# Down projection's last two output blocks in two passes over token halves, with the norm and the index projection by halves

## Chip, core and metric

The kernel runs on one core of one Trainium2 chip. The metric is the device time of one launch in microseconds, the median of several runs. Lower is better.

## What is computed

Two layers of a decoder trunk over 512 tokens of width 1024. Cut to what matters here:

```
for i in range(2):
    h = x @ w_in                      # index, query, key/value, conv and gate projections
    ... three mixers, gates, output projection ...
    x = layer_norm(ALPHA * x + merged @ w_out, ln1_g, ln1_b)
    f_gate, f_up = split(x @ w_ffn_in)            # 1024 -> 2 x 2816
    ffn = (silu(f_gate) * f_up) @ w_ffn_out       # 2816 -> 1024, "down"
    ple = sigmoid(x @ w_ple_gate) * (p_i @ w_ple_proj)
    x = layer_norm(ALPHA * x + ffn + ple, ln2_g, ln2_b)   # "norm 2"
```

All is float32. The norm is over the 1024 channels of a token, so a token's result needs all eight output blocks of the down projection, but no other token.

## The kernel before

**Layout.** The residual `u` and its split copies `xh`, `xl` are held channels on partitions: eight blocks (`DK` = 8) of 128 channels x 512 tokens. Each float32 product is made of three matmuls in the round float format: high x high, high x low, low x high (`three`, L775 to L777; for projections that put tokens on partitions L826 to L828). So every weight is needed as a high and a low part, and every activation too.

**Weight feed.** All weights come as a list of tiles of 128 x 1024 (512 KB), `TILES` = 152 a layer, in the order in which TensorE uses them. SP loads tile t into `wraw[t % 2]` (L411) once POOL is through with tile t-2 (`lo_ready`). ACT rounds it to `wh[t % 4]` (`high`, L489) once TensorE has used tile t-4 (`tile_used`) and the load has landed. POOL makes `wl[t % 4]` = raw - high (`low`, L443), and TensorE waits for that (`arrived`). Each engine runs its list in order. ACT's list has the roundings between its other work: at step k of a stage it rounds the tile three ahead (`LEAD`).

**Down projection.** The 22 input blocks (`FK`) of `hh`, `hl` times the weights of output block j; j runs from 0 to 7. Each j has three tiles (8, 8 and 6 blocks of 128 x 128, the third filled up with zeros), 24 tiles in all. Output block j goes to PSUM bank 2 + j % 2, all 512 tokens at once, and DVE adds it to `u` (`arrive`, L1319).

**Norm 2.** After j = 3 a shift is taken from the first blocks (`shift`, bank 0) and subtracted. DVE keeps a running sum over blocks (L1355), ACT squares each block (`squares`, L578), DVE adds the squares (`add_square`, L1325; both inputs in SBUF). After block 7, TensorE forms per token mean and mean square (`by_token`, L981), spreads the mean to all partitions (L991), DVE and ACT make 1/deviation (`deviation`), DVE puts it on a diagonal (L1379), TensorE spreads it (L995). Then DVE goes through the blocks: scale (L1391, the factor in PSUM), centre (L1367, the mean in PSUM) and, after ACT has made `xh` (`norm_high`, L590), the low part `xl` (L1397, all inputs in SBUF). In the last layer ACT writes the result to `u` (L767) and SP stores each block as it comes.

ACT's squares of blocks 0 to 3 stand in its list at tile step 12 of the down projection; the fourth of them waits for an add of DVE that comes after the sum of block 4.

**Index projection.** The first four tiles of a layer: 2 channel blocks a tile, 452 columns, for all four blocks of 128 tokens, 96 matmuls. TensorE waits for `xl` block by block (`x_ready`).

## Time and profile before

| | us |
|---|---|
| median of 3 runs | 1916.29 (1915.11 to 1917.13) |
| the profiled execution, its own time | 1914.98 |
| its span in the profile | 1913.2 |
| TensorE busy | 1861.6 (97%) |
| VectorE (DVE) busy | 1008.0 |
| ScalarE (ACT) busy | 732.6 |
| GpSimd (POOL) busy | 748.3 |

The profile is of one execution. Times are from the span's start. The median is that of unprofiled runs. A matmul's duration overlaps the next one's, so its pace is read from starts. The granted clock of TensorE is 0.992 of full speed on average. Of DMA, 163.6 MB are weight tiles.

### The profile page before, as it was taken

What the parts mean: (1) busy time and instruction counts of PE and PEld (TensorE: products, weight loads), DVE (VectorE), ACT (ScalarE), POOL (GpSimd) and SP (SyncE); (2) the same over time, 40 slices, a digit from 0 to 9 for tenths busy, and PEclk for the clock granted to TensorE, in tenths of its full rate; (3) what the DMA queues carried; (4) which work ended last, traced back from release to release, by engine and by line L of the source; (5) the groups of instructions that cost most, each with busy time, mean ns of one, the idle gap of its engine ahead of it and who ended that gap; (6) DMA issues with size and microseconds to landing.
All of it is one profiled execution on the core that took longest, in us unless ns stands there. A gap on an engine that the chain in (4) does not pass through costs nothing.

```text
span 1913.2 us, 25744 instructions
## 1 busy us (share of the span) xinstructions
PE 1861.6 (97%) x9076; PEld 1542.2 (81%) x9076; DVE 1008.0 (53%) x1875; ACT 732.6 (38%) x1253; POOL 748.3 (39%) x318
## 2 busy tenths in 40 slices
PE   8999999999999999999999999999999999999996
PEld 8888788878778888887798887888777788888875
DVE  5388777848974121112253987777589731111023
ACT  4544455543242222222344445455433332222222
POOL 4443212234445444443533532222344544444432
PEclk9999999999999999999999999999999999999998
DMA  5322111122233332332332321111132333323322
GB/s 179 100 91 87 45 56 56 56 67 88 89 99 99 99 99 91 97 108 72 121 97 88 100 78 45 56 54 58 56 99 89 110 99 98 97 90 99 103 88 74
DMA packets 47032, 166.07 MB, mean 87 GB/s; under 512 B 5472, under 2 KB 5728, under 8 KB 46944
## 3 DMA queue, kind: packets, MB, share of 16 engines
q1 hardware_dynamic: 46080, 163.60, 27.4%
q10 hardware_dynamic: 864, 1.28, 0.2%
q8 instruction: 58, 0.95, 0.2%
q14 instruction: 30, 0.25, 0.0%
HBM read 162.76 MB, written 2.10 MB: 86 GB/s over the span
## 4 chain that ended last, share of the span: by engine, by line
issue 67%; POOL 28%; PE 2%; POOLq 1%; DVE 1%; DMA 0%; ACT 0%; SPq 0%; DVEq 0%; ACTq 0%
POOL sb_wl L443 28%; PE banks L777 1%; PE banks L775 1%; PE banks L776 1%; POOLq L442 0%; POOLq L452 0%; DMA sb_wraw<-in_weights 0%; DVE sb_u L1391 0%; DMA sb_u<-in_x 0%; DVE sb_u L1367 0%; PE banks L995 0%; PE banks L981 0%; POOL sb_wl L447 0%; ACT sb_u L767 0%; ACT sb_wh L489 0%
## 5 line engine op out<-in xcount | busy, mean ns | idle before, releaser
L443 POOL TENSOR_TENSOR sb_wl<-sb_wraw,sb_wh 128x1024 fp32r<-128x1024 f32 x303 | 745.0, 2462 | 1125.3 <-ACT sb_wh L489 1125.1
L775 PE MATMUL banks<-sb_xh,sb_wh 128*128 128x512 f32 x1344 | 548.0, 408 | 2.8 <-POOL sb_wl L443 1.8
L777 PE MATMUL banks<-sb_xh,sb_wl 128*128 128x512 f32 x1344 | 524.9, 391 | 0.0
L776 PE MATMUL banks<-sb_xl,sb_wh 128*128 128x512 f32 x1344 | 524.4, 390 | 0.0
L489 ACT ACTIVATE sb_wh<-sb_wraw 128x1024 fp32r<-128x1024 f32 x303 | 318.9, 1055 | 263.8 <-PE banks L777 146.9
L777 PEld LDWEIGHTS banks<-sb_xh,sb_wl 128*128 128x128 f32 x1344 | 252.2, 188 | 53.9
L775 PEld LDWEIGHTS banks<-sb_xh,sb_wh 128*128 128x128 f32 x1344 | 253.0, 188 | 51.9 <-issue 5.1
L776 PEld LDWEIGHTS banks<-sb_xl,sb_wh 128*128 128x128 f32 x1344 | 253.5, 189 | 40.0
L1249 DVE SCALAR_TENSOR_TENSOR banks<-sb_hconv,sb_par,banks 128x512 f32<-128x512 f32 x232 | 173.9, 750 | 0.8
L775 PE MATMUL banks<-sb_hh,sb_wh 128*128 128x512 f32 x352 | 138.6, 394 | 2.1 <-POOL sb_wl L443 2.1
L777 PE MATMUL banks<-sb_hh,sb_wl 128*128 128x512 f32 x352 | 138.4, 393 | 0.0
L776 PE MATMUL banks<-sb_hl,sb_wh 128*128 128x512 f32 x352 | 137.3, 390 | 0.0
L1319 DVE TENSOR_TENSOR sb_u<-sb_u,banks 128x512 f32<-128x512 f32 x32 | 21.9, 686 | 201.5 <-PE banks L777 201.3
L1596 DVE TENSOR_TENSOR sb_th<-sb_th,banks 128x512 f32<-128x512 f32 x44 | 30.3, 688 | 175.8 <-PE banks L777 175.8
L1593 DVE SCALAR_TENSOR_TENSOR sb_th<-sb_th,banks 128x512 f32<-128x512 f32 x44 | 30.3, 688 | 158.2 <-ACT sb_th L493 158.2
L534 ACT ACTIVATE sb_ptbuf<-banks 128x128 f32<-128x128 f32 (+3 forms) x128 | 55.9, 437 | 135.7 <-PE banks L882 135.5
L749 ACT ACTIVATE sb_hh<-sb_th 128x512 f32 x44 | 27.8, 632 | 204.1 <-DVE sb_th L1596 204.1
L493 ACT ACTIVATE sb_th<-banks 128x512 f32<-128x512 f32 x60 | 35.9, 598 | 176.0 <-PE banks L777 175.9
L826 PE MATMUL banks<-sb_wh,sb_xh 128*128 128x452 f32 (+3 forms) x256 | 90.3, 353 | 6.2 <-DVE sb_xl L1397 3.5
L827 PE MATMUL banks<-sb_wl,sb_xh 128*128 128x452 f32 (+3 forms) x256 | 90.1, 352 | 0.0
L828 PE MATMUL banks<-sb_wh,sb_xl 128*128 128x452 f32 (+3 forms) x256 | 89.8, 351 | 0.0
L775 PEld LDWEIGHTS banks<-sb_hh,sb_wh 128*128 128x128 f32 x352 | 66.1, 188 | 17.2 <-issue 3.4
(273 smaller groups left out, 2876.9 us busy)
## 6 DMA issues: line engine op xcount, KB each, us to landing
sb_wraw<-in_weights SPq DMA_DIRECT2D x304, 512.0 KB, 3.5
sb_u<-in_x SPq DMA_DIRECT2D x8, 256.0 KB, 6.2
out<-sb_u SPq DMA_DIRECT2D x8, 256.0 KB, 2.0
sb_praw<-in_ple ACTq DMA_DIRECT2D x2, 512.0 KB, 3.9
sb_par<-in_params ACTq DMA_DIRECT2D x2, 98.5 KB, 1.9
sb_rope_tmp<-in_freq ACTq DMA_DIRECT2D x1, 24.0 KB, 4.2
sb_small<-in_pos ACTq DMA_DIRECT2D x1, 2.0 KB, 3.9
```

The source lines that it names most:

```text
L443: nc.gpsimd.tensor_tensor(wl[:, t % WS, :], wraw[:, t % 2, :], wh[:, t % WS, :].bitcast(F32), ALU.subtract).then_inc(lo_ready, 1)
L489: nc.scalar.activation(wh[:, t % WS, :], wraw[:, t % 2, :], ACT.Copy).then_inc(hi_ready, 1)
L493: nc.scalar.activation(dst, psum[:, bank, :], ACT.Tanh, scale=0.5, bias=bias).then_inc(done, 1)
L534: nc.scalar.activation(ptbuf[:, n % 2, 0:w], psum[:, bank, 0:w], ACT.Copy).then_inc(turn_out, 1)
L775: nc.tensor.matmul(out, wh_, xh_, start=start, stop=False)
L776: nc.tensor.matmul(out, wh_, xl_, start=False, stop=False)
L777: return nc.tensor.matmul(out, wl_, xh_, start=False, stop=stop)
L826: nc.tensor.matmul(o, th_, h[:, kk], start=(k == 0), stop=False)
L827: nc.tensor.matmul(o, th_, lw[:, kk], start=False, stop=False)
L828: last = nc.tensor.matmul(o, tl_, h[:, kk], start=False, stop=(k == nk * tiles - 1))
L1249: steps.done(v.scalar_tensor_tensor(acc, h, w, acc, ALU.mult, ALU.add))
L1593: steps.done(v.scalar_tensor_tensor(tc, tc, 1.0, psum[:, 4 + 2 * c, :], ALU.add, ALU.mult))
```

## The change

In each layer the down projection does output blocks 0 to 5 as before (`WHOLE` = 6). Blocks 6 and 7 are done twice over, first for tokens 0 to 255 (22 input blocks for j = 6, 22 for j = 7, 256 columns a matmul), then for tokens 256 to 511. Their weights are in the list twice. Tiles are filled without gaps over the whole list: 220 blocks, 28 tiles, the last with 4 blocks. `TILES` becomes 156.

The second pass uses other banks (4, 5). The norm of half 0 is placed beside it: TensorE has `half_sums` after matmul block 185 and `half_spread` after block 197 of the second pass (blocks 176 to 219). ACT does the half squares at tile steps 20, 22 and 27 of its list, the root at step 23, and the high parts of half 0 two at a time at steps 24 to 27, each behind that step's rounding. DVE goes through half 0 and does the addition of block 6, half 1, in between (`OTHER_AT`). Half 1 follows.

In the second layer the index projection runs by halves, all four tiles for half 0, with the sums and the spread of half 1 after its first and second tile, and then all four tiles, which stay in SBUF, for half 1. The output is stored in 16 pieces.

```diff
+HALVES = 2
+HALF = S // HALVES
+WHOLE = DK - 2
+DOWN = [(j, k, None) for j in range(WHOLE) for k in range(FK)]
+DOWN += [(j, k, half) for half in range(HALVES) for j in range(WHOLE, DK) for k in range(FK)]
+DOWN_TILES = -(-len(DOWN) // DK)
+DOWN_AT = {(j, half): n for n, (j, k, half) in enumerate(DOWN) if k == FK - 1}
+SQUARES_AT = {11: (0, 1, 2, 3), 14: (4,), 17: (5,)}
+HALF_SQUARES_AT = {20: ((6, 0),), 22: ((7, 0),), 27: ((6, 1),)}
+SUMS_AT, SPREAD_AT = DOWN_AT[(DK - 1, 0)] + 10, DOWN_AT[(DK - 1, 0)] + 22
+OTHER_AT = 5
+TILES = T_FO + DOWN_TILES
...
+            for half in range(HALVES):
+                for j in range(DK):
+                    sp.wait_ge(z_full, DK * half + j + 1)
+                    sp.dma_start(out[:, j, columns_of(half)], u[:, j, columns_of(half)]).then_inc(out_stored, 16)
...
-                for k in range(PARTS * DK):
+                for k in range(DOWN_TILES):
                     if T_FO + k + LEAD < TILES or layer < L - 1:
                         high(T_FO + k + LEAD, first)
...
+                    for jj in SQUARES_AT.get(k, ()):
+                        squares(layer, 1, jj)
+                    for j, half in HALF_SQUARES_AT.get(k, ()):
+                        squares_of_half(layer, j, half)
+                    if k == DOWN_TILES - 5:
+                        deviation(layer, 1, 0)
+                    if k >= DOWN_TILES - 4:
+                        for j in range(2 * (k - DOWN_TILES + 4), 2 * (k - DOWN_TILES + 4) + 2):
+                            norm_high(layer, 1, j, 0)
+                squares_of_half(layer, DK - 1, 1)
+                deviation(layer, 1, 1)
                 if layer < L - 1:
                     high(LEAD, first + TILES)
...
+                for j in range(DK):
+                    norm_high(layer, 1, j, 1)
...
+            def index_by_halves(layer, first):
+
+                name, ncol, nk, tiles = TOKEN_GROUPS[0]
+                for half in range(HALVES):
+                    for t in range(tiles):
+                        if half == 0:
+                            arrived(t, first)
...
+                        for kk in range(nk):
+                            k = nk * t + kk
+                            pe.wait_ge(x_ready, split_at(layer - 1, 1, half) + (DK + k + 1))
+                            for b in range(2 * half, 2 * half + 2):
...
+                        if half == 1:
+                            last.then_inc(tile_used, 1)
+                        elif t == 0:
+                            half_sums(layer - 1, 1)
+                        elif t == 1:
+                            half_spread(layer - 1, 1)
...
+            def half_sums(layer, half):
+
+                at, c, blocks = stat(layer, 1, half), columns_of(half), range(2 * half, 2 * half + 2)
+                by_mean, by_square = [psum[:, 2 + 2 * half + i, 0:2] for i in range(2)]
+                pe.wait_ge(sum_ready, at + 1)
+                by_token(by_mean, sums[1][:, 0], blocks).then_inc(mean_ready, 1)
+                pe.wait_ge(sq_half_summed, layer * 2 * HALVES + (2 * half + 2))
+                by_token(by_square, sums[1][:, 1], blocks).then_inc(sq_ready, 1)
+                nc.tensor.matmul(psum[:, STAT[1], c], ones_d[:], sums[1][:, 0, c], start=True,
+                                 stop=True).then_inc(mean_spread, 1)
...
+                for n, (j, k, half) in enumerate(DOWN):
+                    t, c = T_FO + n // DK, slice(n % DK * P, n % DK * P + P)
+                    if n % DK == 0:
+                        arrived(t, first)
...
+                    if half is None:
+                        bank, src_h, src_l = psum[:, 2 + j % 2, :], hh[:, k], hl[:, k]
+                    else:
+                        bank = psum[:, 2 + 2 * half + j % 2, 0:HALF]
+                        src_h, src_l = hh[:, k, columns_of(half)], hl[:, k, columns_of(half)]
+                    last = three(bank, wh[:, t % WS, c], wl[:, t % WS, c], src_h, src_l, k == 0, k == FK - 1)
...
+                    if n == SUMS_AT:
+                        half_sums(layer, 0)
+                    if n == SPREAD_AT:
+                        half_spread(layer, 0)
...
+                    for j in range(DK + 1):
+                        if j < DK:
...
+                            v.scalar_tensor_tensor(u[:, j, c], u[:, j, c], column("l2g", j), scale, ALU.mult,
+                                                   ALU.mult).then_inc(z_ready, 1)
+                            if j + EARLY < DK:
+                                center(j + EARLY)
+                        if j >= 1 and layer < L - 1:
+                            dve.wait_ge(x_high, z0 + (DK + j))
+                            v.scalar_tensor_tensor(xl[:, j - 1, c], u[:, j - 1, c], column("l2b", j - 1),
+                                                   xh[:, j - 1, c].bitcast(F32), ALU.add, ALU.subtract).then_inc(x_ready, 1)
+                        if j == OTHER_AT:
+                            steps.wait()
+                            other()
...
+                add_square(WHOLE - 1)
+                for j in range(WHOLE, DK):
+                    arrive(j, 0)
+                for j in range(WHOLE, DK):
+                    add_square_of(j, 0)
+                chain(0, lambda: arrive(WHOLE, 1))
+                arrive(DK - 1, 1)
+                for j in range(WHOLE, DK):
+                    add_square_of(j, 1)
+                chain(1, lambda: None)
```

## Rows read from the trace of the kernel before

**Rows 1.** The page: busy time of each engine, and POOL's step of the feed.
```profile
PE 1861.6 (97%) x9076; PEld 1542.2 (81%) x9076; DVE 1008.0 (53%) x1875; ACT 732.6 (38%) x1253; POOL 748.3 (39%) x318
...
L443 POOL TENSOR_TENSOR sb_wl<-sb_wraw,sb_wh 128x1024 fp32r<-128x1024 f32 x303 | 745.0, 2462 | 1125.3 <-ACT sb_wh L489 1125.1
```
**Rows 2.** Timeline of TensorE, end of the first layer (start, duration, what, idle before).
```profile
946.22 0.40 PE L777 MATMUL banks<-sb_hh,sb_wl 128*128 128x512 f32 x1
...
950.30 2.05 PE L991 MATMUL banks<-sb_sums,sb_ones_d 128*128 128x512 f32 x2
...
957.63 0.72 PE L826 MATMUL banks<-sb_wh,sb_xh 128*128 128x452 f32 x1 [3.53 <-DVE sb_xl L1397]
...
963.05 0.43 PE L828 MATMUL banks<-sb_wh,sb_xl 128*128 128x452 f32 x1
...
979.69 0.36 PE L828 MATMUL banks<-sb_wh,sb_xl 128*128 128x452 f32 x1
```
**Rows 3.** Timeline of TensorE and DVE, end of the second layer.
```profile
1893.38 0.40 PE L777 MATMUL banks<-sb_hh,sb_wl 128*128 128x512 f32 x1
...
1895.28 1.95 PE L981 MATMUL banks<-sb_ones_d,sb_sums 128*128 128x1 f32 x16 [1.51 <-DVE sb_sums L1355]
...
1897.09 1.11 PE L991 MATMUL banks<-sb_sums,sb_ones_d 128*128 128x512 f32 x2
...
1898.82 2.07 PE L995 MATMUL banks<-sb_sums,sb_ones 128*128 128x512 f32 x2 [0.63 <-DVE sb_sums L1379]
1901.01 0.75 DVE L1391 SCALAR_TENSOR_TENSOR sb_u<-sb_u,sb_par,banks 128x512 f32<-128x512 f32 x1 [1.05 <-PE banks L995]
...
1908.56 1.40 DVE L1391 SCALAR_TENSOR_TENSOR sb_u<-sb_u,sb_par,banks 128x512 f32<-128x512 f32 x2
```
**Rows 4.** Timeline of TensorE, after the tile waits and in a 256-column projection.
```profile
906.53 0.47 PE L775 MATMUL banks<-sb_hh,sb_wh 128*128 128x512 f32 x1 [1.04 <-POOL sb_wl L443]
...
998.00 0.28 PE L826 MATMUL banks<-sb_wh,sb_xh 128*128 128x256 f32 x1
...
1009.51 0.40 PE L826 MATMUL banks<-sb_wh,sb_xh 128*128 128x512 f32 x1
```
**Rows 5.** Timeline of POOL from 900 to 970.
```profile
911.30 2.41 POOL L443 TENSOR_TENSOR sb_wl<-sb_wraw,sb_wh 128x1024 fp32r<-128x1024 f32 x1 [2.55 <-ACT sb_wh L489]
915.14 2.41 POOL L443 TENSOR_TENSOR sb_wl<-sb_wraw,sb_wh 128x1024 fp32r<-128x1024 f32 x1 [1.43 <-ACT sb_wh L489]
...
933.28 2.67 POOL L443 TENSOR_TENSOR sb_wl<-sb_wraw,sb_wh 128x1024 fp32r<-128x1024 f32 x1 [1.07 <-ACT sb_wh L489]
...
968.93 4.88 POOL L443 TENSOR_TENSOR sb_wl<-sb_wraw,sb_wh 128x1024 fp32r<-128x1024 f32 x2 [14.51 <-ACT sb_wh L489]
```
**Rows 6.** Timeline of ACT where it stands before the fourth square.
```profile
902.34 0.63 ACT L578 ACTIVATE sb_sq<-sb_u 128x512 f32<-128x512 f32 x1 [14.46 <-DVE sb_sums L1325]
902.88 1.99 ACT L489 ACTIVATE sb_wh<-sb_wraw 128x1024 fp32r<-128x1024 f32 x2
```
**Rows 7.** Timeline of DVE beside POOL, in norm 2 and norm 1.
```profile
932.99 3.50 DVE L1325 TENSOR_TENSOR sb_sums<-sb_sums,sb_sq 128x512 f32<-128x512 f32 x2
...
533.54 2.40 POOL L443 TENSOR_TENSOR sb_wl<-sb_wraw,sb_wh 128x1024 fp32r<-128x1024 f32 x1 [4.47 <-ACT sb_wh L489]
...
534.47 2.02 DVE L1397 SCALAR_TENSOR_TENSOR sb_xl<-sb_u,sb_par,sb_xh 128x512 fp32r<-128x512 f32 x1
```
**Rows 8.** Stretches of TensorE (busy of PE, PEld, DVE, ACT, POOL, granted clock, DMA).
```profile
958.00:962.00 4.00, 4.00 (x12) 3.51 (x12) 4.00 (x8) 1.45 (x2) 0.00 (x0) 0.50 0.00 0
```
**Rows 9.** Groups of DVE by shape (busy, mean ns, idle before).
```profile
L1325 DVE TENSOR_TENSOR sb_sums<-sb_sums,sb_sq 128x512 f32<-128x512 f32 x28 | 29.5, 1053 | 2.1 <-DVE sb_sums L1325 0.5 <-ACT sb_sq L578 0.2
...
L1319 DVE TENSOR_TENSOR sb_u<-sb_u,banks 128x512 f32<-128x512 f32 x32 | 21.9, 686 | 201.5 <-PE banks L777 201.3
...
L1461 DVE SCALAR_TENSOR_TENSOR sb_scores<-sb_relu,sb_small,sb_scores 128x512 f32<-128x512 f32 x6 | 4.5, 752 | 0.6
...
L1461 DVE SCALAR_TENSOR_TENSOR sb_scores<-sb_relu,sb_small,sb_scores 128x256 f32<-128x256 f32 x6 | 2.9, 485 | 0.6
```

More of the change, by code:

```diff
@@ L959, in attention, with by_token @@
                         turn_blocks("out", n, "", [ystage[:, n % 2, b, :] for b in range(NT)], P)
-            def down(t, part, first, bank, start, stop):
-                arrived(t, first)
-                blocks = min(DK, FK - part * DK)
-                for b in range(blocks):
-                    k, c = part * DK + b, slice(b * P, b * P + P)
-                    last = three(psum[:, bank, :], wh[:, t % WS, c], wl[:, t % WS, c], hh[:, k], hl[:, k],
-                                 start and b == 0, stop and b == blocks - 1)
-                last.then_inc(tile_used, 1)
+            def by_token(bank, block, blocks):
+                for i, b in enumerate(blocks):
+                    last = nc.tensor.matmul(bank[:, i:i + 1], block[:, b * P:b * P + P], ones_d[:, 0:1], start=True,
+                                            stop=True)
+                return last
@@ L1023, in _ @@
                         scratch(n, layer)
+                    elif layer > 0 and n < TOKEN_GROUPS[0][3]:
+                        if n == 0:
+                            index_by_halves(layer, first)
                     elif n in tile_group:
@@ L1115, in _ @@
                         project(T_FI + 2 * c + 1, first + i * 4, xh, xl, DK, [5 + 2 * c])
-                for j in range(DK):
-                    pe.wait_ge(u_ready, layer * 16 + (DK + j + 1))
-                    for part in range(PARTS):
-                        pe.wait_ge(h_done, layer * (DK + FK) + (DK + min(DK * (part + 1), FK) + 2))
-                        down(T_FO + PARTS * j + part, part, first, 2 + j % 2, part == 0, part == PARTS - 1)
-                    if j == 3:
-                        shift(layer, 1)
-                norm(layer, 1)
+                down(layer, first)
+                if layer == L - 1:
+                    half_sums(layer, 1)
+                    half_spread(layer, 1)
         @block.vector
@@ L1351, in norm @@
                     steps.wait()
-                for j in range(4, DK):
+                for j in range(4, (DK, WHOLE)[n]):
                     arrive(j)
@@ L1650, in weight_tiles @@
         tiles += [fi[j:j + 1], fi[FK + j:FK + j + 1]]
-    down = w_ffn_out.reshape(FK, P, DK, P).transpose(2, 1, 0, 3)
-    for j in range(DK):
-        for part in range(PARTS):
-            blocks = down[j, :, part * DK:part * DK + DK]
-            tiles.append(padded(blocks.reshape(1, P, -1)))
+    down = w_ffn_out.reshape(FK, P, DK, P).transpose(2, 0, 1, 3)
+    blocks = [down[j, k] for j, k, _ in DOWN]
+    blocks += [np.zeros_like(blocks[0])] * (DK * DOWN_TILES - len(blocks))
+    tiles.append(np.stack(blocks).reshape(DOWN_TILES, DK, P, P).transpose(0, 2, 1, 3).reshape(DOWN_TILES, P, DK * P))
     return np.concatenate(tiles, axis=0)
```

195 lines of the change are left out of this document (132 added, 63 removed).

## Prediction

> **What bounds the kernel now.** I read first the page's busy times [rows 1]. TensorE is busy 97% of 1913.2 us; no other engine is above 53% (the weight loads lie beside the matmuls). So the time is TensorE's stream of matmuls plus its gaps, and the change can win only gaps. POOL's group waits 1125 us, nearly all on ACT's rounding of a weight tile: it is idle, but it is one link of a chain (load, ACT, POOL), and a chain can be slow although none of its links is busy.
>
> Then the timeline of TensorE at the end of the first layer [rows 2]. The last down matmul starts at 946.22 and ends at 946.62; the index projection starts at 957.63, 3.53 of the 11.0 us between being plain idle there, the rest statistics that wait on one another; it ends at 979.9 (the last starts at 979.69 and the next would follow 0.2 later). Its first 14 steps, to 963.05, are 0.387 us each, the 81 from there to 979.69 are 0.205: the granted clock is 0.50 there, 1.2 of 2.4 GHz [rows 8], and costs 14 x 0.182 = 2.6 us. At the end of the second layer the down projection ends at 1893.78 and the span at 1913.2, so 19.4 us of tail [rows 3]. These two stretches are all that the change can shorten.
>
> **Pace of a half matmul.** Durations overlap, so I take starts. A 512-column matmul comes every 0.229 us (173 steps from 906.53 to 946.22, 0.2283 without the first, which is slower) [rows 2, 4]. A 256-column one comes every 0.1199 us (96 steps from 998.00 to 1009.51, in the projection of the key/value rank) [rows 4]. Two halves cost 0.2398 against 0.2283: 0.0115 x 132 (2 blocks x 22 x 3) = +1.5 us a layer. The Trainium skill (TensorE: Matmul & The Clock Gate, Back-to-back issue gap) gives N/2.4 + 2.5 ns, by which the two would cost 2.5 ns more than the whole, +0.3 us a layer; the rows are of this kernel and decide.
>
> **Pace of the weight feed.** This is where the change meets something that it does not name. A tile goes: load, ACT rounds it, POOL subtracts, and only then may the next load into the same of two buffers be issued. When it is starved the feed shows its own pace [rows 5]: seven POOL steps start between 911.30 and 933.28 (three are shown), 22.0 us for six tiles, 3.66 us a tile, 7.33 us for a round of one buffer. POOL is 2.41 of a round, ACT 1.1 (its two at 902.88 take 1.99 [rows 6]); 3.8 pass from POOL's end to the next rounding in that buffer. A tile of 8 whole blocks lasts 8 x 3 x 0.2283 = 5.48 us, and that pace is covered. A tile of half blocks lasts 8 x 3 x 0.12 = 2.88 us: it is not. The change has 11 such tiles in a row, and 28 tiles instead of 24 (4 more loads, 4 more ACT and POOL steps a layer).
>
> Does it enter with tiles in hand? No. Before, ACT stands 14.5 us in front of the fourth square (it waits for an add that comes after block 4), cannot round, and TensorE then waits 1.04 us for a tile [rows 4, 6]. The change keeps this order: the four squares sit behind tile step 11 instead of 12, block 4 ends at matmul block 111 instead of 109. So TensorE again finds an empty hand, two blocks later: at R = 906.53 + 1.37 = 907.9 (the second layer has the same order, and I take the same for it). I count from R.
>
> **Down stage, step by step from R.** Tiles ready (end of POOL's step, every 7.3 us a buffer): 17 at 7.2, 19 at 14.5, 21 at 21.8, 23 at 29.1, 25 at 36.4, 27 at 43.7; even ones 2.4 us behind (16, 18, ... at 2.3, 9.6, 16.9, 24.2, 31.5, 38.8). TensorE: tile 15 to 5.5; tile 16 (4 whole, 4 half blocks) to 9.7; 17 to 20 to 21.2; waits 0.6 for tile 21 and ends the first pass at 24.7; tile 22 to 27.6; waits 1.5 for tile 23; two blocks of it and the column sums bring it to 30.4. There half_sums waits for the squares. The square of block 7 stands on ACT behind the rounding of tile 25 (step 22), whose load could be issued only when POOL was through with tile 23, at 29.1; it rounds at 32.8 to 33.8, squares to 34.2 (a 512-wide square is 0.63 [rows 6]; I shorten it by what DVE gains, below). Then DVE's add.
>
> That add has both inputs in SBUF, and POOL is just then at tile 25. Rows: two such adds from 932.99 took 3.50 us, while POOL ran 933.28 to 935.95, and one is 0.69 alone; a low-part step took 2.02 beside POOL's at 533.54 (0.74 alone) [rows 5, 7]. They end 0.54 after POOL does. Over the whole kernel the add with two SBUF inputs (L1325) takes 1.053 on average, the one with an input in PSUM (L1319) 0.686, which is never held [rows 9]. The Trainium skill (SBUF — State Buffer, "two separate sides") says the same: a DVE op with two SBUF inputs and a GpSimd op lock each other out for the whole instruction. It speaks against this change, which moves a norm from a stretch where POOL is idle (14.5 us before 968.93 [rows 5]) under a stretch where it works two thirds of the time.
>
> So the add ends at 36.7 and TensorE has stood 6.5 us. Before, the clock had fallen 3.7 us after the last dense matmul in one layer and by 5.1 us in the other (pairs at 950.30 and 1898.82 take 2.05, one at 1897.09 takes 1.11), and it came back after 5.4 us of slow work (957.63 to 963.05) [rows 2, 3]. I take the same here: 2.7 us. Statistics in the stream: by token 16 matmuls took 1.95 us at full clock, so 8 take 1.0; each spread pair took 1.1 at 512 columns, so two half ones 1.0 [rows 3]: 2.0 us.
>
> Down stage then ends at 53.4. Whole: 1.5 + 2.0 + feed waits 2.1 + wait for squares 6.5 + clock 2.7 = +14.8 us against R's old end (946.62 - 907.9 = 38.7). Both layers alike.
>
> **First layer, to the end of the index.** Scale of half 0 lands at 45.5. DVE's loop per block (scale 0.40, centre 0.33, low part 0.40, each 0.27 under the 512 one: 752 against 485 ns [rows 9]) would need 9 us alone. But ACT does blocks 2 and 3 only after the rounding of tile 28, 4 and 5 after tile 29, 6 and 7 after tile 30; these take the feed's pace, and each low part has two SBUF inputs. POOL is at tile 28 until 50.7: low part 2 ends at 51.1; at tile 29 from 51.4 to 53.8: low part 3 ends at 54.2, so scale 5 comes at 54.6 and ACT's block 5 at 55.1, and only then the rounding of tile 30 (to 56.1); POOL is at it until 58.6: low part 5 at 59.0, scale 7 at 59.4, low part 7 at 60.4. DVE then adds block 7 of half 1 and its sum: 61.2. TensorE is through with the first index tile at 55.8: it waits 5.4 us, and the clock falls again (2.7). Then statistics 2.0, 0.5 us of waits, the other 84 index matmuls. Down's end to index's end: 96 x 0.205 = 19.7, + 2.0 + 5.4 + 2.7 = 29.8, against 33.3 before (979.9 - 946.6): -3.5. The second half's low parts (from 70.5, one per 1.13 us) are ahead of TensorE, which takes one per 1.23 us. The rounding behind them (tile 4, at 76.7 to 80.2 with POOL) is just in time for 83.2. Net +14.8 - 3.5 = **+11.3 us**.
>
> **Second layer, tail.** No more loads after tile 27, so POOL is quiet. From down's end to the first scale step: 7.2 before (1893.78 to 1901.01); arrival, sum and diagonal lose 0.27 each, by-token and spread matmuls half their 1.95 and 2.07, part of which DVE's steps hid: 5.0. Then eight scale-centre steps of 1.26 (six from 1901.01 to 1908.56), 9.0 with the last two; 0.53 less each: 5.2. ACT's last step and the store, 3.2 to 1913.2, become 2.9; that SP now issues 16 stores, not 8, I cost at nothing, 0 to +0.5. 13.1 against 19.4 [rows 3]: -6.3. Net +14.8 - 6.3 = **+8.5 us**.
>
> **Sum.** +19.8. The profiled execution was 1914.98 us with a span of 1913.2, 1.3 under the median 1916.29. The sum is made on its span and added to the median: 1936.
>
> **Costed at nothing.** h_done and bank waits of the new loop (other banks, tiles 6 to 20 blocks old); norm 1 (same steps); ACT's copies of the index projection, which come up to 2 us later against their matmuls since a rounding stands before them: covered by the next projections, which TensorE has in hand; without that cover +2. If DVE's steps hold POOL's in turn (its mean is 2.462 over all, 2.41 alone [rows 1, 5]), 0.3 a tile over 11 tiles is +3.
>
> **Rivals.**
> (a) The overlap works as written: the feed keeps up and DVE is not held. Then down ends at 38.7 + 1.5 + 2.0 = 42.2 less rounding, index at 63.6 against 72.0 (-8.4), the tail gives -6.3 + 3.5 = -2.8: -11 us, 1905. It decides if a tile can be fed in under about 3 us; against it speaks every starved step in the rows (3.66), for it only that the first pass might find more tiles in hand than I count. 10%.
> (b) The feed is the bound, but the squares come before the clock falls or the holds on DVE are short: no clock term (-8), shorter waits (-5): +5 to +12, 1921 to 1928. For it: two fifths of the DVE steps will fall into POOL's pauses (3.66 less 2.41), and the clock fell after 3.7 us in one layer and 5.1 in the other, so it has no fixed moment. 23%.
> (c) It evens out: gains of the tails (3.5 + 6.3) equal a down stage that is only 5 us longer, within 4 us: 7%.
> (d) Worse: loads land later, as one did (3.84 us between POOL's steps at 911.30 and 915.14, where the other buffer should have followed by 2.4), the round is 7.7, copies of the index delay the rotation: +24 to +32. 12%.
> (e) Forecast: +12 to +24. 48%.
>
> **How the numbers follow.** Left out of 1918 to 1944 are (a), half of (c) and some of (d), 0.18 in all. The likeliest case's own range is 1928 to 1940. A measurement of this kernel can tell about 0.2% (4 us) from no change. Faster by more: (a), 0.10. Within: (c) and the edge of (b), 0.08. Slower: 0.82.
>
> **What would show it.** Right: TensorE idle 0.5 to 1.5 us before tiles 21 and 23 on POOL's step; 5 to 7 us before the by-token matmuls of the squares, released by DVE; slow matmuls after it; POOL's steps every 3.7 us through both passes; half-width adds and low parts of over 1 us; idle of 3 to 6 us after the first index tile; the tail from the last down matmul 13 us. Wrong: POOL's steps at 3 us, no idle in the second pass, or a down stage under 45 us from R.

## The result

| | median | runs | range |
|---|---|---|---|
| before | 1916.71 us | 4 | 1915.11 to 1921.74 |
| changed | 1936.97 us | 4 | 1934.83 to 1940.31 |

The ratio is 1.0109, 95% interval [1.0095, 1.0123]: 20.3 us slower by the medians. The profiled execution of the changed kernel is the 1940.31 one, with a span of 1938.5 us; the other three have spans of 1936.0, 1934.3 and 1933.0.

From its page: the busy times and the group of POOL's step, to be read beside [rows 1].

```profile
PE 1869.7 (96%) x9348; PEld 1563.3 (81%) x9348; DVE 1034.7 (53%) x1937; ACT 747.6 (39%) x1285; POOL 766.7 (40%) x326
...
L467 POOL TENSOR_TENSOR sb_wl<-sb_wraw,sb_wh 128x1024 fp32r<-128x1024 f32 x311 | 763.3, 2458 | 1146.2 <-ACT sb_wh L513 1146.0
```

TensorE has 272 instructions more, and 8 us more of busy time; the rest of the 25.3 us that this execution is longer is idle. Where it lies, the timeline of TensorE shows (start, duration, instruction, idle before it and its releaser), first layer up to 980, then the second:

```profile
912.19 0.51 PE L811 MATMUL banks<-sb_hh,sb_wh 128*128 128x512 f32 x1 [0.94 <-POOL sb_wl L467]
...
934.33 0.39 PE L811 MATMUL banks<-sb_hh,sb_wh 128*128 128x256 f32 x1 [1.36 <-POOL sb_wl L467]
...
941.59 0.39 PE L811 MATMUL banks<-sb_hh,sb_wh 128*128 128x256 f32 x1 [1.35 <-POOL sb_wl L467]
...
949.00 1.02 PE L1024 MATMUL banks<-sb_ones_d,sb_sums 128*128 128x1 f32 x4 [6.10 <-DVE sb_sums L1426]
...
950.52 0.78 PE L811 MATMUL banks<-sb_hh,sb_wh 128*128 128x256 f32 x1
...
955.78 0.32 PE L813 MATMUL banks<-sb_hh,sb_wl 128*128 128x256 f32 x1
...
965.44 0.28 PE L813 MATMUL banks<-sb_hh,sb_wl 128*128 128x256 f32 x1
965.56 0.37 PE L882 MATMUL banks<-sb_wh,sb_xh 128*128 128x452 f32 x1
...
973.98 1.88 PE L1024 MATMUL banks<-sb_ones_d,sb_sums 128*128 128x1 f32 x8 [5.81 <-DVE sb_sums L1412]
...
995.72 0.35 PE L862 MATMUL banks<-sb_wh,sb_xh 128*128 128x416 f32 x1
```

```profile
1870.84 0.50 PE L811 MATMUL banks<-sb_hh,sb_wh 128*128 128x512 f32 x1 [0.95 <-POOL sb_wl L467]
...
1907.99 1.01 PE L1024 MATMUL banks<-sb_ones_d,sb_sums 128*128 128x1 f32 x4 [5.56 <-DVE sb_sums L1426]
...
1924.49 0.28 PE L813 MATMUL banks<-sb_hh,sb_wl 128*128 128x256 f32 x1
...
1929.13 1.22 PE L1043 MATMUL banks<-sb_sums,sb_ones 128*128 128x256 f32 x2 [1.38 <-DVE sb_sums L1451]
```

Read it as the prediction counts, a stage's end being the start plus the duration of its last matmul: TensorE resumes at tile 15 at 912.19 (R), the last down matmul ends at 965.72, the next projection starts at 995.72; in the second layer R is 1870.84 and the last down matmul ends at 1924.77, 13.7 us before the span does. Between lie, in the first layer, two waits for a tile, one of 6.10 us for the squares, and a wait of 5.81 us after the first index tile. From 950.52 to 955.78 the steps are 0.21 us instead of 0.12. The row of the windows over that stretch (busy of PE, PEld, DVE, ACT and POOL, granted clock, DMA share, GB/s) has half the clock, 1.2 GHz:

```profile
950.00:956.00 6.00, 6.00 (x28) 5.82 (x28) 1.41 (x5) 1.72 (x4) 1.43 (x1) 0.51 0.49 165
```

The 6.10 us are a chain over three engines. POOL, ACT and DVE of the changed kernel, first layer, in that order:

```profile
931.90 2.37 POOL L467 TENSOR_TENSOR sb_wl<-sb_wraw,sb_wh 128x1024 fp32r<-128x1024 f32 x1 [2.26 <-ACT sb_wh L513]
...
939.17 2.37 POOL L467 TENSOR_TENSOR sb_wl<-sb_wraw,sb_wh 128x1024 fp32r<-128x1024 f32 x1 [2.17 <-ACT sb_wh L513]
...
946.32 2.34 POOL L467 TENSOR_TENSOR sb_wl<-sb_wraw,sb_wh 128x1024 fp32r<-128x1024 f32 x1 [2.11 <-ACT sb_wh L513]
```

```profile
945.19 1.06 ACT L513 ACTIVATE sb_wh<-sb_wraw 128x1024 fp32r<-128x1024 f32 x1 [3.40 <-DMA sb_wraw<-in_weights]
946.15 0.40 ACT L608 ACTIVATE sb_sq<-sb_u 128x256 f32<-128x256 f32 x1
```

```profile
946.59 2.36 DVE L1426 TENSOR_TENSOR sb_sums<-sb_sums,sb_sq 128x256 f32<-128x256 f32 x1 [4.76 <-ACT sb_sq L608]
...
961.67 1.92 DVE L1465 SCALAR_TENSOR_TENSOR sb_xl<-sb_u,sb_par,sb_xh 128x256 fp32r<-128x256 f32 x1
...
968.18 2.58 DVE L1412 TENSOR_TENSOR sb_sums<-sb_sums,sb_u 128x256 f32<-128x256 f32 x1
```

A buffer comes round every 7.3 and 7.2 us (931.90, 939.17, 946.32). ACT stands (waits idle) 3.40 us for a load, rounds, and only then squares block 7. DVE's add begins at 946.59, 0.27 after POOL's step at 946.32, and ends 0.3 after it: 2.36 us for 256 columns. The other two DVE rows are held in the same way.

### The profile page after: what moved, and what is told of

The parts are those of the page before. It is cut to its first block, busy times and chain, and to the rows that moved or that the text cites. A ratio compares the mean times of both kernels' runs of the same rounds, so it can differ in the third digit from the quotient of the medians.

```text
span 1938.5 us, 26430 instructions
## 1 busy us (share of the span) xinstructions
PE 1869.7 (96%) x9348; PEld 1563.3 (81%) x9348; DVE 1034.7 (53%) x1937; ACT 747.6 (39%) x1285; POOL 766.7 (40%) x326
## 3 DMA queue, kind: packets, MB, share of 16 engines
q10 hardware_dynamic: 864, 1.28, 0.2%
## 4 chain that ended last, share of the span: by engine, by line
issue 68%; POOL 29%; PE 1%; DMA 1%; POOLq 1%; DVE 0%; ACT 0%; SPq 0%; ACTq 0%; DVEq 0%
POOL sb_wl L467 29%; DMA sb_wraw<-in_weights 0%; POOLq L466 0%; POOLq L476 0%; PE banks L813 0%; PE banks L812 0%; PE banks L811 0%; DMA sb_u<-in_x 0%; DVE sb_sums L1426 0%; DVE sb_u L1436 0%; DVE sb_u L1459 0%; PE banks L1043 0%; PE banks L1024 0%; PE banks L1036 0%; POOL sb_wl L471 0%
## 5 line engine op out<-in xcount | busy, mean ns | idle before, releaser
L467 POOL TENSOR_TENSOR sb_wl<-sb_wraw,sb_wh 128x1024 fp32r<-128x1024 f32 x311 | 763.3, 2458 | 1146.2 <-ACT sb_wh L513 1146.0
L513 ACT ACTIVATE sb_wh<-sb_wraw 128x1024 fp32r<-128x1024 f32 x311 | 327.8, 1056 | 286.7 <-PE banks L813 148.0
L813 PEld LDWEIGHTS banks<-sb_xh,sb_wl 128*128 128x128 f32 x1344 | 252.2, 188 | 53.9
L811 PE MATMUL banks<-sb_hh,sb_wh 128*128 128x512 f32 (+1 forms) x440 | 157.2, 357 | 7.7 <-POOL sb_wl L467 7.7
L813 PE MATMUL banks<-sb_hh,sb_wl 128*128 128x512 f32 (+1 forms) x440 | 154.8, 352 | 0.0
L812 PE MATMUL banks<-sb_hl,sb_wh 128*128 128x512 f32 (+1 forms) x440 | 153.9, 350 | 0.0
L811 PEld LDWEIGHTS banks<-sb_hh,sb_wh 128*128 128x128 f32 x440 | 85.0, 193 | 20.3 <-POOL sb_wl L467 9.4
L812 PEld LDWEIGHTS banks<-sb_hl,sb_wh 128*128 128x128 f32 x440 | 84.9, 193 | 11.9 <-issue 0.5
L813 PEld LDWEIGHTS banks<-sb_hh,sb_wl 128*128 128x128 f32 x440 | 84.9, 193 | 11.1
L862 PE MATMUL banks<-sb_wh,sb_xh 128*128 128x416 f32 (+3 forms) x224 | 78.1, 348 | 3.3 <-POOL sb_wl L467 3.3
```

The lines of the kernel that those rows point to most:

```text
L467: nc.gpsimd.tensor_tensor(wl[:, t % WS, :], wraw[:, t % 2, :], wh[:, t % WS, :].bitcast(F32), ALU.subtract).then_inc(lo_ready, 1)
L513: nc.scalar.activation(wh[:, t % WS, :], wraw[:, t % 2, :], ACT.Copy).then_inc(hi_ready, 1)
L811: nc.tensor.matmul(out, wh_, xh_, start=start, stop=False)
L812: nc.tensor.matmul(out, wh_, xl_, start=False, stop=False)
L813: return nc.tensor.matmul(out, wl_, xh_, start=False, stop=stop)
L862: nc.tensor.matmul(o, th_, h[:, kk], start=(k == 0), stop=False)
```

## The experiments

Ratios are to the kernel before, run beside each group of experiments on the same chip; its medians there were 1916.9 us (runs 1 to 4), 1917.3 (5 to 8), 1917.7 (9 to 11) and 1917.3 (12). One thousandth is 1.9 us; the change itself is at 1.0109 [1.0095, 1.0123]. Differences between runs are taken from the ratios; most carry some 3 to 5 us of uncertainty, so where two intervals overlap it is the trace, not the time, that shows the effect.

**1. The square of block 7 ahead of the rounding.**

```diff
-HALF_SQUARES_AT = {20: ((6, 0),), 22: ((7, 0),), 27: ((6, 1),)}
+HALF_SQUARES_AT = {20: ((6, 0), (7, 0)), 27: ((6, 1),)}
```

> The changed kernel with one edit: the square of block 7, half 0, stands in ACT's list at step 20, beside that of block 6, two roundings earlier than in the change. Theory (ACT's order makes TensorE wait: the square stands behind the rounding of tile 25, which the weight feed lets ACT do only at 34 us after TensorE's resumption): the wait before the by-token matmuls of the squares shrinks from 6.1 us to about 1.6, the clock stays up behind it, a wait of 2 us for the diagonal takes some of it back; -4.5 us in the first layer, -5.5 in the second, about 1927. Rival (the wait is the hold of DVE's add by POOL, whatever ACT's order): the wait stays above 4 us and the time at 1935 to 1937. A second rival, that the squares do not matter since the feed alone sets the pace: the wait goes but comes back before tiles 25 to 27, time 1934 to 1937.

Measured: 1929.25 us, ratio 1.0076 [1.0050, 1.0101], so 6.3 us less than the change, with intervals that just overlap. Timeline of TensorE:

```profile
938.76 0.39 PE L811 MATMUL banks<-sb_hh,sb_wh 128*128 128x256 f32 x1 [1.36 <-POOL sb_wl L467]
...
941.71 0.61 PE L1024 MATMUL banks<-sb_ones_d,sb_sums 128*128 128x1 f32 x4 [1.64 <-DVE sb_sums L1426]
...
943.30 0.41 PE L812 MATMUL banks<-sb_hl,sb_wh 128*128 128x256 f32 x1
...
966.92 1.88 PE L1024 MATMUL banks<-sb_ones_d,sb_sums 128*128 128x1 f32 x8 [6.96 <-DVE sb_sums L1412]
```

The wait for squares is 1.64 us where it was 6.10. Two things take some of it back: the clock, which the expectation held to stay up, fell all the same (0.21 us steps up to 945.65), and the wait after the first index tile grew from 5.81 to 6.96, since TensorE comes there earlier and DVE does not.

**2. The squares of half 0 in PSUM.** DVE's add then has one input in SBUF less; the order stays.

```diff
+dst = psum[:, j % 2, HALF:2 * HALF] if half == 0 else sq[1][:, j % 2, columns_of(half)]
-v.tensor_tensor(squares[:, c], squares[:, c], sq[1][:, j % 2, c], ALU.add)
+v.tensor_tensor(squares[:, c], squares[:, c], src, ALU.add)      # src: the same place as dst
```

> The changed kernel with ACT writing the squares of half 0 to PSUM instead of SBUF, so that DVE's add of them has one input in PSUM; order and sizes as in the change. Theory (the add has two SBUF inputs and is held while POOL subtracts): the two adds take 0.4 us each instead of 2.4, the wait of TensorE before the by-token matmuls of the squares falls from 6.1 us to about 4.1; -2 us a layer, about 1933. If it falls below what drops the clock, up to -5 us more. Rival (the 2.4 us are DVE waiting for something else, such as ACT's write): the adds still take 2.4 us, no change, 1937.

Measured: 1931.57 us, ratio 1.0079 [1.0063, 1.0096]. POOL beside it, DVE's add and the small step behind it, and TensorE's wait:

```profile
941.96 2.34 POOL L467 TENSOR_TENSOR sb_wl<-sb_wraw,sb_wh 128x1024 fp32r<-128x1024 f32 x1 [2.45 <-ACT sb_wh L513]
```

```profile
942.19 0.42 DVE L1427 TENSOR_TENSOR sb_sums<-sb_sums,banks 128x256 f32<-128x256 f32 x1 [6.81 <-ACT banks L609]
...
942.71 1.61 DVE L1441 TENSOR_TENSOR sb_small<-sb_small 128x2 f32<-128x2 f32 x1
```

```profile
942.66 1.01 PE L1024 MATMUL banks<-sb_ones_d,sb_sums 128*128 128x1 f32 x4 [4.21 <-DVE sb_sums L1427]
```

0.42 us against 2.36, beside a step of POOL in both, with only the place of one operand changed: the hold is shown, and it is worth 1.9 us of that wait (1.6 in the second layer, 3.95 against 5.56). The next DVE step with both inputs in SBUF, of two columns, is held in its place (1.61 us; 0.16 in the change). The whole is 5.8 us less than the change where 4 were expected; the intervals just overlap.

**3. The wait filled.** 24 matmuls of 512 columns, whose result nobody reads, between the by-token matmuls of the sum and those of the squares of half 0.

```diff
 by_token(by_mean, sums[1][:, 0], blocks).then_inc(mean_ready, 1)
+if half == 0:
+    for _ in range(24):
+        nc.tensor.matmul(psum[:, 1, :], hh[:, 0, 0:P], hh[:, 0], start=True, stop=True)
```

> The changed kernel with 24 more matmuls of 512 columns (5.5 us at full clock, results not used) put in front of TensorE's wait for the squares of half 0, in both layers. Nothing else moves: TensorE would stand idle there. Theory (the idle of 6 us drops the clock to half and costs 2.7 us behind it): idle falls under 1 us, the granted clock stays at full speed in the second pass, -2.8 us a layer, about 1931.5. Rival (the clock drop costs nothing, since the second pass is paced by the weight feed anyway): 1937. Against both: if the clock drops all the same, the added matmuls run into the path, above 1938.

Measured: 1932.45 us, ratio 1.0077 [1.0060, 1.0094]: 6.1 us less for more work.

```profile
939.36 5.73 PE L1036 MATMUL banks<-sb_hh 128*128 128x512 f32 x24
...
945.75 0.61 PE L1024 MATMUL banks<-sb_ones_d,sb_sums 128*128 128x1 f32 x4 [0.67 <-DVE sb_sums L1429]
...
946.85 0.28 PE L812 MATMUL banks<-sb_hl,sb_wh 128*128 128x256 f32 x1
```

From the by-token matmuls to the next down matmul 0.80 us pass (1.52 in the change), and the steps from 946.85 on are 0.12 at once; the granted clock is at its full level from 938 to 951. The stand is as long, its second price is gone: 3 us a layer.

**4. A short subtraction.** In tiles 16 to 27 POOL subtracts 64 of 1024 columns. The low parts of the other columns are left out, so this is for the time alone; TensorE's instructions are the same.

```diff
-nc.gpsimd.tensor_tensor(wl[:, t % WS, :], wraw[:, t % 2, :], ...)
+nc.gpsimd.tensor_tensor(wl[:, t % WS, 0:n], wraw[:, t % 2, 0:n], ...)      # n = 64 in those tiles
```

> The changed kernel with POOL subtracting only 64 of 1024 columns in down tiles 16 to 27 of each layer; the low parts of the rest of these tiles are left out (what an earlier tile left there is used). POOL's step falls from 2.41 us to about 0.4, a round of a buffer from 7.3 to 5.3 us, 2.6 us a tile, under the 2.88 that a half tile lasts, and POOL no longer holds DVE. Theory (feed pace and hold together are what makes the change slower): no waits for tiles in either pass, no wait for the squares, clock up in the second pass; -11.5 to -12 us a layer, 1913 to 1915. Rival (the passes of 256 columns and the statistics in the stream are what costs): at most -4 us, 1933 or more.

Measured: 1911.65 us, ratio 0.9975 [0.9964, 0.9985]. POOL's step, and TensorE's waits for tiles (us in total, times, longest):

```profile
912.40 0.32 POOL L467 TENSOR_TENSOR sb_wl<-sb_wraw,sb_wh 128x64 fp32r<-128x64 f32 x1 [5.92 <-ACT sb_wh L517]
```

```profile
PE banks L815 <- POOL sb_wl L467: 3.7, 6, 1.0
```

No wait for the squares of half 0 is left, and the waits for tiles are down to 3.7 us (9.6 in the change), none of them within the passes. The time is under the expected 1913 to 1915. One engine at 40% made 25.7 us of difference, by its place in the chain of a tile and by its hold on DVE; this run does not tell the two apart.

**5. The fourth square later, in the change.**

```diff
-SQUARES_AT = {11: (0, 1, 2, 3), 14: (4,), 17: (5,)}
+SQUARES_AT = {11: (0, 1, 2), 14: (3, 4), 17: (5,)}
```

> The change with one edit: ACT's fourth square (block 3, 512 columns) is put behind tile step 14 instead of 11, beside that of block 4. Theory (the halves meet the feed with no tile in hand, because ACT stands about 14 us in front of the fourth square and TensorE finds no tile at tile 15): ACT rounds on in time, two or three tiles are in hand when the half tiles begin, TensorE's 1 us wait before tile 15 and the waits before tiles 21 and 23 are gone, its wait for the squares of the first half is about 3.5 us instead of 6.1, and the clock does not fall there. Down stage about 9 us shorter in each layer, whole kernel about 18 us under the change: 1919 us (1915 to 1924), ratio to the kernel before 1.001. Rival (the pace of the feed under half tiles sets the time whatever it enters with): it catches up within the 11 half tiles, the waits move but their sum does not change, 1932 to 1937.

Measured: 1924.44 us, ratio 1.0031 [1.0019, 1.0043]: 15.0 us under the change, where 18 were expected.

```profile
937.86 1.01 PE L1024 MATMUL banks<-sb_ones_d,sb_sums 128*128 128x1 f32 x4 [4.14 <-DVE sb_sums L1426]
...
942.51 0.39 PE L812 MATMUL banks<-sb_hl,sb_wh 128*128 128x256 f32 x1
```

All waits for tiles in the passes are gone. What was missed: the wait for squares is 4.1 and 4.6 us, not 3.5, and the clock fell after it (0.21 us steps up to 942.72). Fourteen such steps (1.5 us) and slower statistics (0.7, as in 3) are 2.2 us a layer, and the longer waits 0.6 and 1.1: 6.1 us in all, more than the 3.0 that are missing by the ratios and near the 5.4 by the medians.

**6. The same square later, in the kernel before.**

```diff
-for jj in range(4) if j == 4 else range(j - 1, j):
+for jj in range(3) if j == 4 else range(3, 5) if j == 5 else range(j - 1, j):
```

> The kernel before with the same edit alone: its fourth square behind tile step 15 instead of 12. Theory: ACT's stand of 14 us in front of it, and TensorE's wait of 1.04 us for a tile that follows from it, are gone in both layers, and nothing else was waiting there: about 2 us under the kernel before, 1914.7 us, ratio 0.9989. Rival: TensorE's wait only moves to the next tile, ratio 1.0000; or the square comes too late for the column sums and the end of the down projection waits, ratio above 1.001.

Measured: 1912.87 us, ratio 0.9980 [0.9971, 0.9989]. ACT in front of that square, to be read beside [rows 6]:

```profile
903.73 0.63 ACT L578 ACTIVATE sb_sq<-sb_u 128x512 f32<-128x512 f32 x1 [3.33 <-DVE sb_sums L1325]
```

The stand of 14.46 us is 3.33, and TensorE's two waits of a microsecond are gone. The ratio says 3.8 us, where 2 were expected; the span is 2.9 shorter. In the trace 2.1 are the waits, 1.2 come from 8 index matmuls at half clock where 14 were, and some is lost again in the second layer, where the by-token matmuls took 2.38 us (1.95 before).

**7. Both orders.** The edits of 1 and 5 together.

> Both orders on ACT together: the fourth square behind tile step 14, and the square of block 7's first half behind step 20 instead of 22. By the theory each mends the same stretch (what TensorE waits for at the end of the second pass's eighth block), so they do not add: 1918.5 us, within 2 us of the one with the fourth square alone; TensorE's wait for the squares is under 1 us, and about 3 us of wait for the diagonal stand in its place, since DVE's steps are still held by POOL. If they were independent, their gains (about 8 us for the order alone) would add to about 1911.

Measured: 1920.89 us, ratio 1.0017 [1.0006, 1.0029]. They do not add: 17.6 us, not 15.0 + 6.3. TensorE, then ACT and DVE:

```profile
943.46 0.70 PE L1043 MATMUL banks<-sb_sums,sb_ones 128*128 128x256 f32 x2 [3.02 <-DVE sb_sums L1451]
```

```profile
939.65 1.06 ACT L513 ACTIVATE sb_wh<-sb_wraw 128x1024 fp32r<-128x1024 f32 x1 [3.02 <-DMA sb_wraw<-in_weights]
940.72 1.28 ACT L616 ACT_TABLE_LOAD   x1
```

```profile
942.44 0.17 DVE L1449 RECIPROCAL sb_small<-sb_small 128x2 f32<-128x2 f32 x1 [5.44 <-ACT sb_small L618]
```

The expectation put the wait for the diagonal down to POOL's hold. The row says otherwise: DVE stood 5.44 us for ACT's deviation (L616, L618). That stood behind the rounding of step 23, for whose load ACT had waited 3.02 us, and 1.28 us of it are a load of the activation table.

**8. The index projection whole.**

```diff
-elif layer > 0 and n < TOKEN_GROUPS[0][3]:
-    if n == 0:
-        index_by_halves(layer, first)
...
-if layer == L - 1:
-    half_sums(layer, 1)
-    half_spread(layer, 1)
+half_sums(layer, 1)
+half_spread(layer, 1)
```

> The change with the index projection whole: the column sums, the norm and the spread of the second half come directly behind the down projection in the first layer too, as they do in the second, and index tile 0 comes after them with 512 columns. The output is the same. Theory: index by halves hides 5 us of DVE's work (tail of the first half's norm, sums of the second) behind the 12 matmuls of index tile 0, the rest of the gain is that the second norm has a whole tile less to feed behind it: whole, down's end to index's end is about 10 us longer, 1947 us (1943 to 1950), and the down stages are unchanged. Rival (TensorE would wait the same for the sums either way, the stall is only moved in front of the index tile): 1936 to 1939.

Measured: 1947.99 us, ratio 1.0166 [1.0150, 1.0182], 11 us over the change: the wait for the sums is longer, and two follow it that were hidden.

```profile
967.75 1.88 PE L1024 MATMUL banks<-sb_ones_d,sb_sums 128*128 128x1 f32 x8 [7.29 <-DVE sb_sums L1408]
...
973.93 1.22 PE L1043 MATMUL banks<-sb_sums,sb_ones 128*128 128x256 f32 x2 [3.23 <-DVE sb_sums L1447]
...
977.26 0.72 PE L862 MATMUL banks<-sb_wh,sb_xh 128*128 128x452 f32 x1 [2.11 <-DVE sb_xl L1461]
```

So this part of the change is worth having, given the halves.

**9. The deviation a step earlier.** On top of 7.

```diff
-if k == DOWN_TILES - 5:
+if k == DOWN_TILES - 6:
     deviation(layer, 1, 0)
-if k >= DOWN_TILES - 4:
-    for j in range(2 * (k - DOWN_TILES + 4), 2 * (k - DOWN_TILES + 4) + 2):
+if DOWN_TILES - 5 <= k < DOWN_TILES - 1:
+    for j in range(2 * (k - DOWN_TILES + 5), 2 * (k - DOWN_TILES + 5) + 2):
```

> The halves as well as the order on ACT can place them: both orders of the run before (fourth square behind tile step 14, both half squares of the first half behind step 20), and in addition the deviation of the first half behind step 22 instead of 23 and its eight high parts behind steps 23 to 26 instead of 24 to 27. Theory: in the run with both orders TensorE still waited 3.1 us a layer for the diagonal and the clock fell after it, because ACT's deviation stood behind a rounding; one step earlier that wait and the slow matmuls after it are gone and the last low parts of the first half no longer stand in front of the sums. About 3 us a layer less than 1920.9: 1915 us (1912 to 1918), no faster than the kernel before with its own fourth square moved (1912.9). Rival: the diagonal is late because DVE is held by POOL and not because of ACT, so the wait stays at 3 us and the time at 1920 to 1922.

Measured: 1911.64 us, ratio 0.9979 [0.9967, 0.9991]. DVE before the reciprocal, then the longest wait of TensorE that is left:

```profile
936.01 0.17 DVE L1449 RECIPROCAL sb_small<-sb_small 128x2 f32<-128x2 f32 x1 [2.02 <-ACT sb_small L618]
```

```profile
953.91 1.01 PE L1024 MATMUL banks<-sb_ones_d,sb_sums 128*128 128x1 f32 x4 [3.40 <-DVE sb_sums L1412]
```

No wait is left within the passes of the first layer, and of the two waits for the diagonal in the second pass (3.02 and 3.08 us in 7) none. It gained 7.3 us more than 7 by the ratios, where 6 were expected: the place of ACT's deviation was the cause, and not POOL's hold. The high parts moved with it, and what they alone give is not shown. With three placements on ACT changed (fourth square, square of block 7, deviation) the change's loss is gone, and it is level with 6, which is the kernel before with one square moved.

**10. The short subtraction and the fourth square.** The edits of 4 and 5 (low parts left out as in 4, so for the time alone).

> What the halves could give at best: the fourth square behind tile step 14, and POOL subtracts 64 of the 1024 columns of each tile of the half blocks (the low parts of those weights are left out, so this is for the time only), so that neither the feed nor POOL's hold on DVE costs anything. TensorE's instructions are the same. Theory: what is left of the change is +1.5 us of narrower matmuls and +2 us of statistics in the stream a layer, against tails that are 3.5 + 4.9 us and 6.3 us shorter; 2 us under the run with the short subtraction alone (its 1 us stand at tile 15 is gone in both layers): 1909.5 us (1907 to 1911), ratio 0.996, so 3 us under the kernel before with its own fourth square moved. Rival: with the holds gone the tails give more than I count, below 1905.

Measured: 1909.23 us, ratio 0.9956 [0.9942, 0.9971]. As expected: 8.4 us under the kernel before by the ratio, and no rival's further gain. It is not the bound that the expectation calls it, since one wait is left:

```profile
954.75 1.45 PE L1028 MATMUL banks<-sb_ones_d,sb_sums 128*128 128x1 f32 x6 [4.85 <-DVE sb_sums L1416]
```

It comes after the first index tile, and the clock fell behind it. The intervals of this run and of 11 and 12 lie on one another.

**11. The kernel before, with 6's edit and its stands filled.**

```diff
+busy(6)
 pe.wait_ge(sum_ready, layer * 2 + (n + 1))
...
+busy(3)
 pe.wait_ge(diag_ready, layer * 2 + (n + 1))
 nc.tensor.matmul(scale, ones_1[:], sums[n][:, 1], start=True, stop=True).then_inc(spread, 1)
+if layer == 0:
+    busy(14)
```

> The kernel before with its fourth square moved, and besides matmuls whose result nobody reads in the norm that ends each layer: 6 of 512 columns ahead of the wait for the sums, 3 ahead of the wait for the diagonal, and in the first layer 14 between the spread and the index projection. The output is the same. Theory (the slow matmuls after sparse statistics are the price of the stands, not of the statistics themselves): TensorE's clock stays at 2.4 GHz, the spread pairs take 1.1 instead of 2.0 us and the first nine index matmuls 0.205 instead of 0.37 us each; about 2.3 us in the first layer and 0.9 in the second: 1909.7 us (1908 to 1912), ratio 0.9965. Rival: the granted clock falls all the same, or the matmuls stand in the way of the statistics for longer than they save: 1912.5 to 1915.

Measured: 1912.29 us, ratio 0.9961 [0.9949, 0.9974]. Fillers, spread pairs and the first index matmul, to be read beside [rows 2], and the windows over the statistics:

```profile
949.49 2.27 PE L987 MATMUL banks<-sb_hh 128*128 128x512 f32 x3
951.56 1.53 PE L1001 MATMUL banks<-sb_sums,sb_ones 128*128 128x512 f32 x2
...
956.62 0.44 PE L826 MATMUL banks<-sb_wh,sb_xh 128*128 128x452 f32 x1 [0.31 <-DVE sb_xl L1405]
```

```profile
948.80:950.50 1.70, 1.70 (x5) 0.82 (x5) 1.03 (x3) 1.24 (x2) 0.00 (x0) 0.61 0.00 0
950.50:952.50 2.00, 2.00 (x6) 1.19 (x5) 1.28 (x2) 0.00 (x0) 1.95 (x1) 0.50 0.00 0
```

No index matmul runs at half clock, as expected. But the expectation that the clock stays up was half wrong: behind the sixteen one-column matmuls it fell to 1.2 GHz all the same, before 950.5, and stayed there until 952.5, and the spread pairs take 1.69 and 1.53 us, not 1.1; the second layer shows the same. At that clock the three fillers ahead of the diagonal take 2.1 us and stand in its way: the last spread pair starts 6.48 us after the start of the last down matmul, 5.65 in run 6, and the first index matmul 11.5 us after it (945.08 to 956.62), 10.9 in run 6. The ratio is the expected one, 3.6 us under that of 6, yet the median is above the expected range, 0.6 under that of 6, and the intervals overlap: what it gains over 6 is not settled.

**12. The halves of 9 with its stands filled.** 7, 13 and 8 such matmuls in the first layer, 4 and 5 in the second.

> The halves with both orders and the earlier deviation, and besides matmuls of 512 columns whose result nobody reads in front of the stands that were left: in the first layer 7 ahead of the first index tile, 13 ahead of the sums of the second half, 8 ahead of its squares; in the second layer 4 ahead of the sums and 5 ahead of the diagonal. The output is the same. Without them TensorE stood 1.9, 3.4 and 2.0 us in the first layer and ran the index projection at half the clock up to 963.8. Theory (the stands' second price is the clock): the stands become busy time of the same length, the thirteen index matmuls take 0.205 instead of 0.38 us each (2.3 us) and the statistics 1.2 us less: 3.5 us under the run without them, 1908 us (1906 to 1910), ratio 0.9960. Rival: it stays at 1911 to 1913, ratio 0.998, because the sums of the second half end with DVE's steps, which the clock of TensorE does not move.

Measured: 1909.87 us, ratio 0.9962 [0.9948, 0.9976]. The span is 1906.1 where that of 9 is 1909.2, the mean clock 0.998 where it was 0.994. That is the expected ratio, and no matmul of norm 2 runs at half clock in either layer. It is 3.3 us under 9 by the ratios and 1.8 by the medians, with overlapping intervals, so the times alone do not settle what filling gives here; it is 0.0001 from run 11, and the fastest of the halves with nothing left out. One row of the second layer bears on the clock:

```profile
1879.47 0.61 PE L1026 MATMUL banks<-sb_ones_d,sb_sums 128*128 128x1 f32 x4 [1.09 <-DVE sb_sums L1437]
```

Here TensorE stood 1.09 us between the same statistics as in run 1, with no wait for a tile before it, and the clock stayed up (1.00 from 1877 to 1885).

## Why the prediction was right

**The sum.** Against each execution's own start of the stretch, since the profiled one was 4.3 us behind at R (2.0 of them since its first 40 us, the rest since norm 1 of the first layer, in code that the change does not touch; the other spans are 2.5 to 5.5 us shorter):

| | forecast | measured |
|---|---|---|
| down stage from R, first layer | 53.4 | 965.72 - 912.19 = 53.5 |
| same, second layer | 53.4 | 1924.77 - 1870.84 = 53.9 |
| waits for tiles in the passes | 0.6, 1.5 | 1.36, 1.35; second layer 1.15, 1.98 |
| wait for the squares | 6.5 | 6.10, 5.56 |
| round of a buffer | 7.3 | 7.2 to 7.3 |
| wait after the first index tile | 5.4 | 5.81 |
| down's end to index's end | 29.8 | 995.72 - 965.72 = 30.0 |
| net to the end of the index | +11.3 | (995.72 - 4.3) - 979.9 = +11.5 |
| tail of the second layer | 13.1 | 13.7 |
| net of the second layer, from R | +8.5 | +9.5 |
| whole | +19.8 | +20.3 by the medians |

That the down stage agrees to a tenth is in part luck, because four errors cancel. The half matmuls were costed too high: the first 107 steps (920.57 to 932.69) are 0.1133 us each, not 0.12, which is 0.7 us. So TensorE was early at tile 21 and its two waits are 2.7 us, not 2.1, as the feed sets the pace there. The wait for the squares is 0.4 us shorter and the clock 0.4 dearer than forecast. The stretch to the index's end leaves out of its sum the 0.5 us of waits that the text beside it names.

**The feed.** That the half tiles would run at the feed's pace and that TensorE would enter them with an empty hand is shown by 4 and 5: with the subtraction short, or the hand full, the waits within the passes go. How much hung on the entry was not in the prediction: it named the stand before the fourth square as why the hand is empty, but treated it as given, and moving that one instruction took 15 of 20 us.

**The hold on DVE.** Forecast as an add held until 0.5 us after POOL's step, and run 2 shows it by the operand's place. The Trainium skill (SBUF — State Buffer, "two separate sides") has it that of a DVE step with two SBUF inputs and a GpSimd step that reads SBUF, whichever starts first keeps a shared port to itself until it is done. The trace agrees: POOL began at 946.32, the add at 946.59, and it took 2.36 us against 0.42 with one input in PSUM. Which steps would be held was forecast less well than the sum of it: the low part of block 2 was held as forecast, that of block 3 was not, that of block 4 and the sum of block 6 were instead, and the last low part of half 0 ended 60.9 us after R, 60.4 forecast.

**The clock.** Forecast 2.7 us a stand. Measured 3.1 in the first layer against run 3: 0.7 in the statistics (1.52 against 0.80 us), 2.4 in some 23 matmuls. It is shown by 3. Where the text was wrong is its condition: rival (b) let the clock stay up if the stand was short, and the expectations of run 1 (1.6 us) and run 5 (3.5 us) counted on that. In run 1 it fell after 1.64 us of idle and the sparse statistics around it, with a wait for a tile of 1.36 us that had ended 3 us before.

**The tail.** It is 0.6 longer than forecast: the first scale step comes 5.6 us after down's end, not 5.0. The rows of ACT and DVE show where:

```profile
1927.51 0.30 ACT L618 ACTIVATE sb_small<-sb_small 128x2 f32<-128x2 f32 x1 [1.74 <-DVE sb_small L1444]
```

```profile
1927.79 0.75 DVE L1436 TENSOR_TENSOR sb_u<-sb_u,banks 128x256 f32<-128x256 f32 x2 [0.31 <-PE banks L1036]
1928.46 0.16 DVE L1449 RECIPROCAL sb_small<-sb_small 128x2 f32<-128x2 f32 x1
```

The changed kernel has DVE centre two blocks ahead of the reciprocal; the one before does it behind the diagonal, while TensorE spreads. ACT's deviation was there at 1927.81, and the reciprocal came 0.65 us later. Neither the description of the change nor the prediction has this, and no run tests it. The tail's eight steps (5.3) and its end (2.8) are as worked out.

**The rivals.** (a) fell as the kernel stands. What 9 and 12 show is that it fell by the order on ACT and not by the pace of the feed alone: the same loads, tiles and matmuls, ordered otherwise, are 4 us under the kernel before, where (a) said 11. The fastest run (10) is 8.4 us under it, and it still has a wait of 4.85 us after the first index tile, which (a) counts as none. (b) fell since the clock did fall and the holds were not short. (c) and (d) did not come, nor did the two terms costed at nothing with a price: POOL's mean step is 2458 ns, 2462 before.

**What the change is worth.** Its intended gain is there: the tails are 3.3 us (33.3 against 30.0) and 5.7 us (19.4 against 13.7) shorter. But 6 gets the like of 9, and 11 the like of 12, without the second pass; two halves with everything in place and whole blocks with everything in place cannot be told apart here.

## What to carry to other kernels

Narrower tiles of work ask more of whatever feeds them: before cutting a matmul's columns in two, divide the time of a tile by the time of a round of the feed's buffer, and look at how many tiles are in hand where the narrow ones begin. On an in-order engine that both feeds and computes, an instruction that waits for something late (here one square, then one deviation) holds all feeding behind it; put it where its input is ready, and do that before restructuring. Count a stand of TensorE twice where the clock falls in it: its length, and the slow matmuls after it.

## What the runs showed of the hardware

- The granted clock fell to half after stands much shorter than the rows of before suggested: 1.64 us of idle with statistics around it and a tile wait of 1.36 us shortly before (run 1), 3.02 us (run 7, 0.21 us steps up to 947.5). After 1.09 us with the same statistics and no tile wait before (run 12, second layer) it did not fall.
- With matmuls of 512 columns in the stands of runs 3 and 12 the stream went on at full pace. In run 11 the clock fell to half for some 3.5 us although six of them stood in the first stand: sixteen one-column matmuls came behind them.
- The hold between POOL and DVE is paid by DVE, as far as the rows show: POOL's steps in the second pass are 2.34 to 2.54 us long and average 2458 ns in the kernel, 2462 in the one before, while DVE's held ones take 1.92 to 2.58 us for 0.42 to 0.48 of work. In the held rows shown here POOL had begun first.
- POOL's subtraction of 64 columns takes 0.32 us, of 1024 columns 2.4.
